# Delta rule: first output half added by token block, VectorE's second weight split moved behind TT

## What is computed

```python
decay = jnp.exp(jnp.where(causal, gc[..., :, None] - gc[..., None, :], -jnp.inf))
a_low = jnp.where(strict, jnp.einsum('bhnid,bhnjd->bhnij', k_beta, k) * decay, 0.0)
t_inv = lax.linalg.triangular_solve(eye + a_low, eye, left_side=True, lower=True, unit_diagonal=True)
u = t_inv @ (v * beta[..., None])
w = t_inv @ (k_beta * jnp.exp(gc)[..., None])
attn_intra = jnp.einsum('bhnid,bhnjd->bhnij', q, k) * decay
...
o = o * lax.rsqrt(jnp.mean(o * o, axis=-1, keepdims=True) + RMS_EPS) * norm_g
o = o * jax.nn.silu(z)
x = x + o.reshape(bsz, seq, B_V_DIM) @ w_o
```

## Time and profile before

| | |
|---|---|
| median of 3 executions | 1564.29 us (1562.88 to 1564.59) |
| profiled execution | 1563.21 us |
| its span | 1561.4 us |
| TensorE busy | 1512.3 us, 97% |
| VectorE, ScalarE, GpSimd busy | 547.4, 377.7, 184.2 us |
| DMA | 450.4 MB, 288 GB/s over the span |
| granted TensorE clock, mean | 0.994 |

### The profile page before, as it was taken

The page is one execution under the profiler, slowest core; times in us unless marked ns, Lnnn a source line. Parts: engine busy times, 40 slices in busy tenths (PEclk is TensorE's granted clock), DMA queues, the critical chain, the costliest instruction groups (busy, mean ns, idle before and its releaser), DMA issues.

```text
span 1561.4 us, 35145 instructions
## 1 busy us (share of the span) xinstructions
PE 1512.3 (97%) x15735; PEld 870.0 (56%) x15735; DVE 547.4 (35%) x763; ACT 377.7 (24%) x604; POOL 184.2 (12%) x182
## 2 busy tenths in 40 slices
PE   9999999999999998997999999999999999999997
PEld 7778888777777786732434434344344244344344
DVE  5754455485857666412110111011021011101221
ACT  5554344564645463201000000000000000000000
POOL 0100000134433325101001001000010010010000
PEclk9999999999999999999999999999999999999998
DMA  9336555542232305578999999999999999999991
GB/s 344 102 130 229 191 184 188 189 153 91 80 111 72 118 1 217 198 277 331 409 402 421 412 411 420 410 415 419 408 417 420 408 418 415 407 421 415 410 421 55
DMA packets 113099, 450.40 MB, mean 288 GB/s; under 512 B 11136, under 2 KB 42400, under 8 KB 82240
## 3 DMA queue, kind: packets, MB, share of 16 engines
q1 hardware_dynamic: 109424, 437.10, 71.5%
q0 software_dynamic: 3536, 11.14, 1.8%
HBM read 440.87 MB, written 7.34 MB: 287 GB/s over the span
## 4 chain that ended last, share of the span: by engine, by line
PE 87%; DVE 9%; ACT 1%; issue 1%; DMA 1%; POOL 1%; SPq 0%; POOLq 0%; ACTq 0%; DVEq 0%
PE banks L2031 37%; PE banks L2046 19%; PE banks L1522 8%; PE banks L1524 7%; PE banks L1523 7%; DVE cvall L1210 3%; DVE wlo L1012 2%; PE banks L1951 1%; PE banks L1941 1%; PE banks L1932 1%; DMA raw<-in_attn_w_qkv_dram 1%; DVE T L1270 1%; PE banks L1989 1%; PE banks L1651 1%; PE banks L1960 0%
## 5 line engine op out<-in xcount | busy, mean ns | idle before, releaser
L2031 PE MATMUL banks<-ring,xg 128*32 128x512 f32 (+1 forms) x6144 | 582.5, 540 | 8.5 <-DVE ehid L1345 8.5
L2031 PEld LDWEIGHTS banks<-ring,xg 128*32 128x32 f32 x6144 | 186.4, 110 | 392.2 <-issue 378.9
L2046 PE MATMUL banks<-ring,ehT 128*32 128x256 f32 x5376 | 292.9, 379 | 0.0
L1345 DVE TENSOR_TENSOR ehid<-banks,esil 64x1536 f32<-64x1536 f32 (+1 forms) x32 | 79.6, 2487 | 569.1 <-ACT esil L941 568.9
L2046 PEld LDWEIGHTS banks<-ring,ehT 128*32 128x32 f32 x5376 | 162.4, 110 | 132.3 <-issue 7.7
L1012 DVE TENSOR_TENSOR wlo<-raw,whi 128x2048 fp32r<-128x2048 f32 x74 | 179.9, 2432 | 79.4 <-ACT whi L690 79.3
L941 ACT ACTIVATE esil<-banks 64x1536 f32<-64x1536 f32 (+1 forms) x32 | 39.4, 1277 | 666.1 <-PE banks L2031 666.1
L1522 PE MATMUL banks<-whi,xhi 128*128 128x512 f32 x448 | 182.4, 407 | 5.8 <-DVE X L1196 2.8
L1524 PE MATMUL banks<-whi,xlo 128*128 128x512 f32 x448 | 175.2, 391 | 0.0
L1523 PE MATMUL banks<-wlo,xhi 128*128 128x512 f32 x448 | 174.9, 390 | 0.0
L690 ACT CAST whi<-raw 128x2048 fp32r<-128x2048 f32 x74 | 141.1, 1907 | 48.6 <-PE banks L1524 44.3
(11 more groups left out here) (314 smaller groups left out, 1250.2 us busy)
## 6 DMA issues: line engine op xcount, KB each, us to landing
ring<-in_moe_w_down_dram SPq DMA_DIRECT2D x112, 1024.0 KB, 8.7
ring<-in_moe_w_gate_dram SPq DMA_DIRECT2D x64, 1024.0 KB, 10.0
ring<-in_moe_w_up_dram SPq DMA_DIRECT2D x64, 1024.0 KB, 10.7
ring<-in_moe_w_gate_dram SPq DMA_DIRECT2D x64, 768.0 KB, 7.5
ring<-in_moe_w_up_dram SPq DMA_DIRECT2D x64, 768.0 KB, 8.6
raw<-in_dn_w_in_dram SPq DMA_DIRECT2D x16, 1024.0 KB, 5.1
raw<-in_ffn_w_gate_dram SPq DMA_DIRECT2D x22, 512.0 KB, 3.9
raw<-in_ffn_w_up_dram SPq DMA_DIRECT2D x22, 512.0 KB, 4.9
```

The source lines that it names most:

```text
L1345: i = dve.tensor_tensor(ehid[64 * s:64 * s + 64, 0:TILES * n_].rearrange("p (t k j) -> p t k j", t=TILES, k=k_), by_row(products, s), by_r ...
L2031: p_ = pe.matmul(bank[2 * t + s][TILE * q:TILE * (q + 1), 0:n_], xg[:, t, k, :], w[q // 2][:, s, q % 2, :], start=k == 0, stop=k == KT - 1)
L2046: i = pe.matmul(token_tile(6, t, q, 256), ehT[c][:, h_:h_ + TILE], w[:, at_:at_ + 256], start=c == 0 and m == 0 and k == 0 and t % 2 == 0, ...
```

## The change

Three things are done in the group's loop. The first half's adds are written per block (`add_block`), each with its own increment of `outputs_added`: block 0 waits for `block0_psum`, which TensorE now increments for that half too, and block 1 for the panel. TensorE waits for each bank apart (`i < 2`), and the counts follow (4 instead of 3 increments per group). `ahead(1)` moves from ahead of `A` to behind `TT`, right ahead of `ahead(2)`.

```diff
-        QK_BLOCK0, OUT_BLOCK0 = (1, 2, 3, 5), (4, 6, 7)
+        QK_BLOCK0, OUT_BLOCK0 = (1, 2, 4, 7), ((3, 5), (6, 8), (9, 10))
...
             def add_second_outputs(g, b):
-                dve.wait_ge(*((panel_used, WO[g, 1] + 1) if b else (sem("block0_psum"), OUT_BLOCK0[g])))
-                s_ = X[:, b, 512:]
+                add_block(g, 1, b)
+
+            def add_block(g, h, b):
+                dve.wait_ge(*((panel_used, WO[g, h] + 1) if b else (sem("block0_psum"), OUT_BLOCK0[g][h])))
+                s_ = X[:, b, h * 512:(h + 1) * 512]
                 dve.tensor_tensor(s_, s_, bank[6 + b], ALU.add).then_inc(sem("outputs_added"), 1)
...
                 ahead(0)
                 if g:
-                    add_outputs(g - 1, 0, lambda b, h: 6 + b).then_inc(sem("outputs_added"), 1)
-                ahead(1)
+                    for b in range(TB):
+                        add_block(g - 1, 0, b)
...
                         .then_inc(sem("TT0_ready"), 1)
+                ahead(1)
                 ahead(2)
...
-                if i == 0 and g and 0 in steps:
-                    pe.wait_ge(*((sem("z_ready"), 1) if g == 1 else (sem("outputs_added"), 3 * (g - 2) + 1)))
+                if i < 2 and g and 0 in steps:
+                    pe.wait_ge(*((sem("z_ready"), 1) if g == 1 else (sem("outputs_added"), 4 * (g - 2) + i + 1)))
...
-                    elif h == 1 and g + 1 < GROUPS:
+                    elif g + 1 < GROUPS:
                         i_.then_inc(sem("block0_psum"), 1)
...
-                    elif i == 2:
-                        pe.wait_ge(sem("outputs_added"), 3 * g + 1)
+                    else:
+                        pe.wait_ge(sem("outputs_added"), 4 * g + i - 1)
```

More of the change, by code:

```diff
@@ L1770, in project @@
                 first_v = g == 0 and m in (2, 3)
-                if i == 0 and g and 0 in steps:
-                    pe.wait_ge(*((sem("z_ready"), 1) if g == 1 else (sem("outputs_added"), 3 * (g - 2) + 1)))
+                if i < 2 and g and 0 in steps:
+                    pe.wait_ge(*((sem("z_ready"), 1) if g == 1 else (sem("outputs_added"), 4 * (g - 2) + i + 1)))
                 if i in (4, 5) and 0 in steps and not first_v:
-                    pe.wait_ge(*((sem("prj_qk_ready"), 2 * g + i - 3) if g < 2 else (sem("outputs_added"), 3 * (g - 2) + i - 2)))
+                    pe.wait_ge(*((sem("prj_qk_ready"), 2 * g + i - 3) if g < 2 else (sem("outputs_added"), 4 * (g - 2) + i - 1)))
                 if i == 8 and 0 in steps:
@@ L1992, in _ @@
                     i.then_inc(sem("o_psum"), 1)
-            pe.wait_ge(sem("outputs_added"), 3 * (GROUPS - 1))
+            pe.wait_ge(sem("outputs_added"), 4 * (GROUPS - 1))
             keep_clock(14, bank[6])
```

## The result

| | before | after |
|---|---|---|
| median of 8 executions | 1564.44 us | 1569.18 us (1566.78 to 1572.92) |
| ratio | | 1.0027, 95% interval 1.0018 to 1.0037 |
| profiled execution | 1563.21 us | 1567.53 us |
| its span | 1561.4 us | 1565.7 us |
| granted clock, mean | 0.994 | 0.990 |

The change makes the kernel slower by 0.27% (4.2 us by the ratio, 4.7 us by the medians). In its eight executions the mean granted clock lies between 0.987 (the slowest, 1572.92 us) and 0.991 (the fastest, 1566.78 us).

The account below looks back on a forecast made before the run. VectorE's work from the first split to Pc was taken to bound the stretch. Work of 1.2 - 0.2 - 0.2 + 0.0 = +0.8 us plus one clock fall of 1.5 gave +2.3, some 1566.5 us; range about 1561.5 to 1569.0 us.

Parts of the forecast that it names:

- the case that I had given 0.22: Clock falls in groups 0 and 3 and stays down through group 3's chain: +3.8 to +5.3 us, chance 0.22.
- The work: Delta rule, first split to Pc, all four groups, clock effects left out: +0.8 us in sum.
- VectorE binds the stretch: First split to Pc is VectorE's work; 8.4 us of TensorE's waits for X, T, TT become longer waits for Pc.
- Group 0, +1.2 us: Two splits behind TT take 6.3 us beside ktail; TensorE's L1951 starts at 359.7 against 358.50, 1.2 us later.
- Groups 1 and 2, -0.2 us each: Two splits end at 433.45 in group 1, Pc at 433.67, 0.2 us earlier; group 2 the same.
- Group 3, 0.0: VectorE idles 1.0 us before TT, which ends at 598.3; Pc starts at 604.0, as before.
- The wait for the moved panel: Groups 1 and 2: TensorE waits some 0.5 us for the moved split's panel, inside the wait for Pc.
- The clock: Gaps before Pc in groups 0 and 3: even odds of a fall at each, one fall costing 1.5 us.
- Under 2.5 us never: Gap ahead of L1951: the clock always falls with gaps over 4.4 us in both groups, never under 2.5 us.
- The splits not lengthened by GpSimd: Splits behind TT take 2.29 us each despite GpSimd, and the clock holds: -5.6 us, 1558.7 us, chance 0.12.
- The full promise: All 8.4 us of TensorE's waits for X, T and TT are gained: 1555.9 us, chance 0.04.

Follow-up runs that it names:

- ktail later: The whole change, with GpSimd's two ktail products moved behind its last copy of Ac, against the kernel before: 1563.64 us, ratio 0.9992.
- the third split a level later: The whole change, with the third split moved from between TT and Pc to later levels, against the kernel before: 1555.27 us, ratio 0.9940.
- add with spares: Only the add by block, with eight spare matmuls ahead of T's transposes in groups 1 to 3, against the kernel before: 1564.84 us, ratio 0.9998.
- ten spares: The whole change, with ten spare matmuls ahead of L1951 in level 1 of groups 0 and 3, against the kernel before: 1565.06 us, ratio 1.0005.
- the add alone: Only the add by block with the bank handed over, second split still ahead of A, against the kernel before: 1566.63 us, ratio 1.0013.
- the split alone: Only the second split moved behind TT, first-half adds kept together with one increment, against the kernel before: 1570.45 us, ratio 1.0037.
- the last but one: The whole change with the third split later, but in group 3 back between TT and Pc, against the kernel before: 1559.06 us, ratio 0.9958.

## Why the prediction was right or wrong

The forecast was 1566.5 us, slower by 0.15%; measured were 1569.18 us by the median of its runs, which is 0.2 us past the upper end of the range, and 1568.5 us by the ratio on the median that I started from, which is inside it. That the stretch is VectorE's, and that the long wait at its end brings the clock down, held. The size was too small: +2.3 us against 4.2, and what came was nearest to the case that I had given 0.22, with falls at both places.

Two terms of the sum were off, in opposite directions, and partly hid each other. The work was to cost 0.8 us and saved 0.3; the clock was to cost 1.5 us and cost 3.6. So the sign of the forecast is right by the clock alone: without its falls the change is worth nothing or a little, not a loss.

- **VectorE binds the stretch: right.** The waits for X and `T` went and one for `Pc` took their place, 10.7 us where I had said about 10. The gaps were 3.68, 1.59, 1.59 and 3.80 us against 3.8, 1.5, 1.5 and 3.5.
- **Group 0, +1.2 us: right, measured +1.01.** A waited for the products of k (1.03 us), the mask caught T again, and the two splits took 6.23 us (6.3 taken).
- **Groups 1 and 2, -0.2 us each: measured -0.42 and -0.41. Group 3, 0.0: measured -0.46.** So the sum of the work was -0.3 us, not +0.8. In group 3 some 0.15 us of the miss is TT, which ended 13.18 us behind the start of `vb` (13.33 taken; VectorE idled 0.70 us ahead of it instead of 1.0), and the rest is mostly the two splits, 5.57 us where I had taken 5.8.
- **The wait for the moved panel**, 0.5 us taken, was 0.93 us, and lay ahead of the wait for Pc inside the same stretch, as said.
- **The clock: the term that was mis-sized.** I gave each place even odds and 1.5 us. Both fell, for 2.4 and 1.25 us. I took the price from spare matmuls that were at the lower level for 3.4 us. In group 3 it was down for as long, and the price was about right; in group 0 it was down for 6.8 us (357.6 to 364.5), 5.3 us of it with TensorE at work. The case with 0.22 had it the other way round, with the long fall in group 3's chain. The odds were too low: in the delta rule the clock fell behind every one of the eleven pauses of 2.13 us or more in these traces (four of 2.13 to 2.15 us ahead of `T`, in the two runs with the adds by block and the second split ahead of A; 2.35 and 3.13 us with ktail later; 3.65 to 3.82 us in the rest). "Under 2.5 us never" was wrong.
- **The splits not lengthened by GpSimd, with 0.12**: fell for this change, 6.23 us for two. But the reading that ruled it out was wrong. I took the split of 430.55, 0.01 us ahead of `ktail` and yet 3.19 us long, as a sign that the first to start is not spared. The rows taken one by one say that one of the two is spared, and within 0.01 us the start doesn't say which. Nor does every split beside a GpSimd product take 2.9 to 3.25 us: the one of 382.89 takes 2.29.
- **The full promise** fell for this change, but the third split a level later reached it.

What stays open is how short a pause can be that still brings the clock down. Between 1.4 and 1.9 us one trace has a fall where another has none. Behind a pause of 1.84 us in layer 0, which all twelve traces have, it fell twice (near 116 us); behind the eight of 1.53 to 1.60 us it fell once (1.53 us, add with spares); and it fell once behind 1.42 us (ten spares).

## What to carry to other kernels

Where TensorE's small waits all sit on one engine's stretch of work, moving a piece of that work within the stretch doesn't remove a wait: it gathers the waits at the stretch's end. Gathered, they can be long enough to lower the clock: here the moved waits by themselves cost nothing (-0.3 us), and the clock 3.6 us. What pays is to take work out of the stretch (here the third split, to a level with slack, and GpSimd's product from beside the splits). Until then a gap of over 2 us is worth filling with spare matmuls, and nearly whole: of a wait of 3.7 us ten of them left 1.42 us and the clock still fell in the traced execution, fifteen left 0.26 us and it held.

## What the runs showed of the hardware

- With the add alone, TensorE waited 2.13 us, did eight transposes with a wait of 0.40 us among them, and was then at 1.2 GHz for 3.4 us; the same again in group 2.
- A fall costs by how long the clock is down while TensorE works. The falls here lasted 3.4, 6.8 or 10.2 us. In group 0, where dense steps follow, 3.4, 5.3 and 6.8 us at work at the lower level cost 1.54, 2.38 and 3.10 us (ten spares, the change, the split alone), about 0.45 us for each us. In group 3's chain of levels 3.4, 3.4, 5.6 and 10.2 us cost 1.25, 1.20, 2.04 and 3.71 us (the change, add with spares, group 3 of the last but one, the split alone), about 0.36 us for each us.
- A split takes 2.29 us alone. Beside a GpSimd product that gets ahead of it, it takes 3.19 us and the product its 1.04; where the split gets ahead, it takes 2.29 us and the product 3.1 to 3.2. Beside the 2.4 us mask, started 0.7 us behind it, a split takes 3.85 us. Two splits in a row take 6.23 us beside two products of `ktail` and a copy of `Ac`, and 4.90 us beside a copy alone.
